# Gate, residual and mean of a layer norm moved into the matmul phases ahead of it

## What is computed

```python
def deepnorm_residual(x, delta, gate, g, b):
    return layer_norm(DEEPNORM_ALPHA * x + gate * delta, g, b)

def layer_norm(x, g, b):
    mu = jnp.mean(xf, axis=-1, keepdims=True)
    var = jnp.mean(jnp.square(xf - mu), axis=-1, keepdims=True)
    return ((xf - mu) * lax.rsqrt(var + LN_EPS)).astype(x.dtype) * g + b

def squared_relu_mlp(h, w_fc1, w_fc2):
    return jnp.square(jax.nn.relu(h @ w_fc1)) @ w_fc2
```

## Time and profile before

| | us |
|---|---|
| median of 3 runs | 5848.92 |
| lowest, highest | 5848.59, 5851.17 |
| the profiled execution | 5849.96 |
| span of its profile | 5848.2 |
| busy: PE, PE's weight loads | 5231.4, 4740.4 |
| busy: DVE, ACT, POOL | 2408.4, 1883.7, 592.0 |

### The profile page before, as it was taken

The page is one execution under the profiler, slowest core; times in us unless marked ns, Lnnn a source line. Parts: engine busy times, 40 slices in busy tenths (PEclk is TensorE's granted clock), DMA queues, the critical chain, the costliest instruction groups (busy, mean ns, idle before and its releaser), DMA issues. The chain is left out here.

```text
span 5848.2 us, 148613 instructions
## 1 busy us (share of the span) xinstructions
PE 5231.4 (89%) x66464; PEld 4740.4 (81%) x66464; DVE 2408.4 (41%) x4332; ACT 1883.7 (32%) x3891; POOL 592.0 (10%) x1104
## 2 busy tenths in 40 slices
PE   6797999988998897999896897899897999988998
PEld 2386888877997876999795776799786888877997
DVE  0242554534334264433324543433452545544334
ACT  1032343433223254222423432322322443433223
POOL 0002232300000000000002221000001232310000
PEclk8798999988998898999897998899898999988999
DMA  9731000011221301221222111122121000011221
GB/s 405 325 116 47 23 15 25 15 57 53 78 72 50 73 2 51 80 72 57 94 99 69 42 36 70 58 73 73 40 104 58 24 15 25 15 43 63 75 72 54
DMA packets 99124, 411.81 MB, mean 70 GB/s; under 512 B 17947, under 2 KB 33691, under 8 KB 68830
## 3 DMA queue, kind: packets, MB, share of 16 engines
q1 hardware_dynamic: 87014, 376.71, 18.5%
q10 hardware_dynamic: 11520, 26.22, 1.1%
HBM read 358.20 MB, written 39.44 MB: 68 GB/s over the span
## 5 line engine op out<-in xcount | busy, mean ns | idle before, releaser
L375 PE MATMUL bank<-src_hi,ring_hi 128*128 128x320 f32 x4032 | 933.1, 313 | 156.8 <-DVE ring_lo L356 58.5
L375 PE MATMUL bank<-src_hi,ring_lo 128*128 128x320 f32 x4032 | 927.1, 311 | 4.0 <-issue 4.0
L375 PE MATMUL bank<-src_lo,ring_hi 128*128 128x320 f32 x4032 | 928.6, 312 | 0.0
L375 PEld LDWEIGHTS bank<-src_hi,ring_hi 128*128 128x128 f32 x4032 | 682.5, 190 | 164.8 <-issue 152.5
L375 PEld LDWEIGHTS bank<-src_hi,ring_lo 128*128 128x128 f32 x4032 | 683.1, 190 | 4.2 <-issue 4.2
L375 PEld LDWEIGHTS bank<-src_lo,ring_hi 128*128 128x128 f32 x4032 | 683.8, 190 | 0.0
L589 ACT ACTIVATE stage<-bank 128x320 f32<-128x320 f32 x512 | 196.1, 435 | 1388.8 <-PE bank L375 1388.8
L367 DVE TENSOR_TENSOR ring_lo<-ring,ring_hi 128x2048 fp32r<-128x2048 f32 x178 | 407.5, 2290 | 519.2 <-ACT ring_hi L363 518.3
L375 PE MATMUL bank<-hidden_hi,ring_hi 128*128 128x320 f32 x2048 | 466.6, 309 | 0.0
L375 PE MATMUL bank<-hidden_hi,ring_lo 128*128 128x320 f32 x2048 | 466.6, 309 | 0.0
L375 PE MATMUL bank<-hidden_lo,ring_hi 128*128 128x320 f32 x2048 | 466.6, 309 | 0.0
(11 more groups left out here) (401 smaller groups left out, 8613.9 us busy)
## 6 DMA issues: line engine op xcount, KB each, us to landing
ring<-w_mlp SPq DMA_DIRECT2D x128, 1024.0 KB, 4.9
mod_ring<-w_mod SPq DMA_DIRECT2D x48, 2048.0 KB, 11.9
ring<-rw_wrkv SPq DMA_DIRECT2D x22, 1024.0 KB, 5.2
rkv<-stage ACTq DMA_DIRECT2D x48, 320.0 KB, 2.2
ring<-dn_win SPq DMA_DIRECT2D x15, 1024.0 KB, 5.2
r_k<-rkv SPq DMA_DIRECT2D x32, 320.0 KB, 3.5
dn_proj<-stage ACTq DMA_DIRECT2D x32, 320.0 KB, 2.2
src<-mixed SPq DMA_DIRECT2D x24, 320.0 KB, 7.3
```

The costliest lines, as they stand in the source:

```text
L375: last = self.nc.tensor.matmul(acc[h][:, 0:HALF], wt[:, n % 2, k, m * P:(m + 1) * P], x[:, k, h * HALF:(h + 1) * HALF], start=first and q ...
```

## The change

1. **Out projection.** A function of its own, `out_projection`, takes the place of `projection` there. It is written out without a loop. ACT gates each unit straight from its banks into `delta`, in three pieces (320, 192 and 128 tokens); DVE forms the residual of the unit at once (`joined`); PE has the mean product of unit u - 2 behind product u. Two pairs of banks hold the units instead of four; two more banks hold the mean and stay until the norm has read them.
2. **Mlp.** The last quarter leaves the loop. In its second half ACT gates block u - 9 behind the evacuation of unit u, DVE joins block u - 10 behind the add of unit u, and PE has the mean product of block u - 10 behind product u. Here too two pairs of banks instead of four.
3. **Norm.** It begins with the subtraction of the mean. A root of one column (`warm`) stands first on ACT, so that the table is loaded there. The memsets, the rounding of the first slab and the two halves of its rest move behind the root, the reciprocal and the scaling.

The parts that carry the work (in the norm, the gates at L684, the residual at L738 and the mean products at L712 are deleted):

```diff
+class Residual:
...
+    def joined(self, past, b):
+        x = self.g.x[:, b, :]
+        return self.nc.vector.scalar_tensor_tensor(x, x, ALPHA if self.first else past[:, b:b + 1], self.delta[:, b, :], ALU.mult, ALU.add)
+
+    def mean_product(self, b):
+        for (cols, n), mean in zip(((S_LAT, LAT), (S_CTX, CTX)), self.mean):
+            self.nc.tensor.matmul(mean[:, 0:n], self.g.mean_w, self.g.x[:, b, cols], start=(b == 0), stop=(b == NB - 1))
+
+def out_projection(nc, g, w, delta, layer, mean, load):
...
+            @block.tensor
+            def _(pe):
+                def means(b):
+                    pe.wait_ge(s["joined"], b + 1)
+                    residual.mean_product(b)
...
+                            last = ring.product(acc[u % DEEP], n, m, k, x_hi, x_lo, k == 0, k == NB - 1)
+                        last.then_inc(s["mm_done"], 1)
+                        if u >= 2:
+                            means(u - 2)
+                for b in range(NB - 2, NB):
+                    means(b)
...
+                        act.wait_ge(s["mm_done"], u + 5)
+                        front, back = acc[u % DEEP]
+                        residual.gated(delta[:, u, 0:HALF], front[:, 0:HALF], past, u, 0)
+                        residual.gated(delta[:, u, HALF:LAT], back[:, 0:in_half], past, u, 0)
+                        residual.gated(delta[:, u, LAT:T], back[:, in_half:HALF], past, u, 1).then_inc(s["evacuated"], 1)
...
+                    for u in (2 * n, 2 * n + 1):
+                        dve.wait_ge(s["evacuated"], u + 1 + DEEP)
+                        residual.joined(past, u).then_inc(s["joined"], 1)
+def mlp(nc, g, w, delta, held, layer, mean):
...
                             last.then_inc(s["mm_done"], 1)
+                            if final and u >= NB + 2:
+                                means(u - NB - 2)
...
+                block_(LAST, False, True)
+                for b in range(NB - 2, NB):
+                    means(b)
...
                             last.then_inc(s["evacuated"], 1)
-
-                with act.Fori(0, QUARTERS - 1) as i:
+                            if not more and u > NB:
+                                gate(u - NB - 1)
...
                                 nc.vector.tensor_tensor(delta[:, u - NB, :], delta[:, u - NB, :], row,
                                                         ALU.add).then_inc(s["added"], 1)
+                                if not more and u >= NB + 2:
+                                    join(u - NB - 2)
...
@@ norm @@
+                nc.scalar.activation(warm[:, :], g.eps_ln, ACT.Sqrt).then_inc(s["warm"], 1)
                 for b in range(NB):
                     act.wait_ge(s["centred"], b + 1)
                     nc.scalar.activation(dl[:, b, :], g.x[:, b, :], ACT.Square).then_inc(s["squares"], 1)
                 act.wait_ge(s["variances"], 1)
                 nc.scalar.activation(dev[:, :], var[:, 0:W], ACT.Sqrt, bias=g.eps_ln).then_inc(s["deviation"], 1)
+                if held:
+                    act.wait_ge(s["w_first"], 16)
+                    nc.scalar.copy(hi, raw).then_inc(s["w_upper"], 1)
```

More of the change, by code:

```diff
@@ L451, in _ @@
                 for b in range(NB):
[L452 to L456, removed]
+                    for ap, cols in token_parts(g.h, b):
                         last = nc.scalar.copy(x_hi[:, b, cols], ap)
                     last.then_inc(s["hi_ready"], 1)
[L459 to L465, removed]
+                    if b in (2, 3):
+                        ring.upper_first(act, (FRONT, BACK)[b - 2])
                 def block_(i, more):
@@ L523, in mlp @@
+def mlp(nc, g, w, delta, held, layer, mean):
     QUARTERS, PER = NFB // NB, 8
-    names = SPLIT_SEMS + ["cleared", "added", "link", "hidden"]
-    PASS_UNITS = 2 * PER
+    names = SPLIT_SEMS + ["cleared", "added", "link", "hidden", "past_cols", "gated", "joined"]
+    PASS_UNITS, DEEP, LAST = 2 * PER, 2, QUARTERS - 1
+    residual = Residual(nc, g, delta, layer, 1, mod_at(layer, 5), mean)
     with buffers(nc) as (sb, banks), phase(nc, *names) as s:
@@ L530, in mlp, with _ @@
         stage = sb("stage", 2, T)
-        bank = banks(8)
-        acc = [(bank[2 * u], bank[2 * u + 1]) for u in range(UNITS)]
+        past = sb("past", 2 * NB)
+        bank = banks(2 * DEEP)
+        acc = [(bank[2 * u], bank[2 * u + 1]) for u in range(DEEP)]
         with nc.Block() as block:
+            @block.gpsimd
+            def _(pool):
+                residual.past_columns(past).then_inc(s["past_cols"], 1)
             @block.sync
@@ L575, in _, with gate @@
                     last.then_inc(s["hi_ready"], 1)
+                def gate(b):
+                    act.wait_ge(s["added"], NB * QUARTERS + b + 1)
+                    for c, cols in enumerate((S_LAT, S_CTX)):
+                        last = residual.gated(delta[:, b, cols], delta[:, b, cols], past, b, c)
+                    last.then_inc(s["gated"], 1)
                 def block_(i, more):
@@ L607, in _, with join @@
                 dve.wait_ge(s["cleared"], 1)
+                def join(b):
+                    dve.wait_ge(s["gated"], b + 1)
+                    residual.joined(past, b).then_inc(s["joined"], 1)
                 def block_(i, more):
@@ L709, in _ @@
                 for b in range(NB):
-                    pe.wait_ge(s["added"], b + 1)
-                    for cols, mean, n in parts:
-                        last = nc.tensor.matmul(mean[:, 0:n], g.mean_w, g.x[:, b, cols], start=(b == 0), stop=(b == NB - 1))
-                last.then_inc(s["sums"], 1)
-                for b in range(NB):
                     pe.wait_ge(s["squares"], b + 1)
@@ L733, in _ @@
                 last.then_inc(s["chosen"], 1)
-                if not first:
-                    dve.wait_ge(s["past_cols"], 1)
-                for b in range(NB):
-                    dve.wait_ge(s["gated"], b + 1)
-                    nc.vector.scalar_tensor_tensor(g.x[:, b, :], g.x[:, b, :], ALPHA if first else past[:, b:b + 1], dl[:, b, :],
-                                                   ALU.mult, ALU.add).then_inc(s["added"], 1)
-                dve.wait_ge(s["sums"], 1)
-                for b in range(NB):
-                    for cols, mean, n in parts:
-                        last = nc.vector.tensor_tensor(g.x[:, b, cols], g.x[:, b, cols], mean[:, 0:n], ALU.subtract)
-                    last.then_inc(s["centred"], 1)
+                dve.wait_ge(s["deviation"], 1)
+                nc.vector.reciprocal(dev[:, :], dev[:, :]).then_inc(s["root"], 1)
                 if held:
```

199 lines of the change are left out of this document (133 added, 66 removed).

## The result

The changed kernel took 5883.7 us (median of 5 runs, 5873.2 to 5886.7) beside 5848.6 of the kernel before on the same chip: a ratio of **1.0055, 95% interval 1.0043 to 1.0068**, 32 us slower. The profiled execution took 5886.7 us, its span is 5884.5, 36.3 us more than in the profile of before.

The account below looks back on a forecast made before the run. TensorE, busy 89% of the span, was taken as the bound. The eight norms' 125.1 us became 42.0 (out projections) plus 128.8 (mlps), +45.7, less 4.8 for jumps: +41 us, so 5890 us, range 5862 to 5915.

Parts of the forecast that it names:

- the clock: Mlp last quarters: TensorE's clock halves after two stalls in three, 1.1 us a stall, 6.6 us a norm (0 to 10.2).
- the switches: TensorE changing between products and mean weights: 12 a norm, between 0 and 2.3 us, taken as 0.4 us a norm.
- the stall with the product behind it: Mlp: 2.61 us of idle TensorE at each of six units, plus a 1.08 us mean product; five before the last product.
- the jumps: Mlp loops: four jumps back instead of eight leave one gap of two, -4.8 us (bounds -9.6 to +9.6).
- Output projection: Four out projections with their norms: no wait between units, 5.4 + 4.5 = 9.9 us a norm; 20 us won.
- The tail: From a phase's last product to the end of its mean: 4.5 us in the out projection, 6.8 us in the mlp.
- the gate in three pieces: ScalarE's gate of the out projection's last unit from its banks: 1.5 us, bounds 0.77 to 1.65.
- Neither bound: Mlp clock loss: 0 to 1.7 us a stall, from no fall (5864, chance 0.13) to every stall halving it (5905).
- The table load: Norms behind the out projections: early load wins 0.43 us, but squares start 0.6 us later; net +0.2 us each.
- do not catch up: Same four norms: squares starting 0.6 us late stay late, at 0.79 us each with VectorE feeding at 0.81.
- The moved work: Norm and mlp: moved cast of first weights, five memsets and two accumulators instead of four cost nothing.
- The rival that the mlp is covered too: Mlp: join of unit u - 2 done before product u ends, 11.7 us a norm, 5808 us; chance 0.05.

Follow-up runs that it names:

- one moved line: Changed kernel with the mlp's mean product one unit later, 5802.8 us; or with VectorE's join ahead of its wait for the new unit, 5803.0 us.

## Why the prediction was right, point by point

The forecast was 5890 us within 5862 to 5915; the measured time is 5883.7, the measured difference 32 us (25 to 40) where 41 were forecast, just above its interval. The mechanism is the one forecast: the same stalls, in the same number, at the same place. The sizes are in part off, and in part they cancel. Set against the 36.8 us of the stages, the clock and the switches were put 9 us too high, the stall with the product behind it 3.5 and the jumps 2 us too low.

- **Output projection**: forecast 20 us won (21 by its stage, less the table), measured 19.9. The tail was forecast at 4.5 us and is 4.5 to 4.8; the gate in three pieces takes 1.37 us, in the bounds and near the 1.5 taken. It didn't wait between its units.
- **The stall in the mlp**: forecast 2.61 us at six units of four norms, some 62 us in all; measured 2.51 and 60.2. VectorE's add and join overlap, 0.74 us from start to start and not 0.85. But the distance of the evacuations is 10.90 us, not the 10.7 forecast: a stalled mean product adds 3.86 us to its unit, where 2.61 + 1.08 = 3.69 were forecast. A pause of 2.51 us so costs 0.27 more than its length. In the records 0.10 of that is in the mean product itself (1.35 us long at 1833.07, 1.24 at 1342.52 in the output projection, where nothing pauses); the rest is that matmuls which follow each other overlap (those of a unit are 0.31 us long and 0.15 apart), and the last one ahead of a pause has none to overlap with. The tail was forecast at 6.8 us and is 6.84 in two norms; in the two others a half clock in it makes it 8.5.
- **The clock**: two falls in three were taken, one in two is measured: 12 of 24, 4.7 us a norm and not 6.6. Filling the stall removed all of them, which shows that the idle time is their cause. Neither bound came, no fall or a fall each time. With the mlps alone changed it was 9 of 24, so the share is itself not a fixed one, and 6.6 was a middle between bounds and not a mechanism. The rule of the Trainium skill, TensorE: Matmul & The Clock Gate, section on psum-queue depth-cycling, is that micro-idles between groups of matmuls make the clock fall and rise. By the trace it holds in kind, but not for every stall, and not at all for pauses of 1.3 us.
- **Switches**: forecast 0.4 us a norm; the output projection's units are 8.12 us apart, which leaves nothing for them.
- **The table load**: forecast 0.2 us lost in each of four norms, measured 0.43 won. The step that failed is "do not catch up": 0.79 us a square was VectorE's pace, not ScalarE's. Back to back they start 0.62, 0.63 and 0.68 us apart, and with the fourth they have caught up. The page ScalarE: Activation LUTs of the Trainium skill, section What ACT_TABLE_LOAD costs, has back-to-back instructions overlap by about 0.09 us, and the trace agrees (0.72 long, 0.62 to 0.63 apart in the first ones). Its 2.66 us for a switch is seen in no run here; where the load stands ahead of the root, squares, load and root follow each other within 0.03 us.
- **The jumps**: one gap at the jumps was forecast for 4.8 us less; there was one, but it cost 6.8 us in place of the 9.6 of the two before, so 2.8 us less. That it was one was luck: taking a rate from two gaps of one program was the weak step, for four other programs had none, and the one with the output projections alone had two, each of two pauses of 1.1 to 1.4 us.
- **The moved work** (first slab, memsets, two pairs of banks) cost nothing, as forecast: from the root to the scaling the norms take 4.24 us as before, and from there to the mlp's first product 12.6.

The rival that the mlp is covered too gave 5808 us. It isn't what the changed kernel does, but it is what one moved line makes of it: 5802.8 and 5803.0.

## What to carry to other kernels

When work is woven into another engine's queue, it isn't its own inputs that count but what stands ahead of them in the queue of the engine that makes them: here a residual whose gated input was ready one unit before (its gate ended at 1832.44, the next evacuation began at 1841.50) came 2.5 us late because it was made behind the newest unit. Take from the producer's queue only what it finished before the consumer's current unit began, one unit of lag more, or put the old work ahead of the wait for the new. And count a pause of TensorE above its length: each of 2.5 us here cost 0.27 us more and, in nearly half of the cases, 1.5 to 1.7 us of clock.

## What the runs showed of the hardware

- A pause of 2.51 us in dense products brought TensorE's clock down 12 times of 24 in the changed kernel and 9 times of 24 with the mlps alone changed; one of 1.34 us at the same places 0 times of 24, and one filled with needless products 0 times of 24. A fall is 3.4 us at 1.2 GHz and cost 1.5 to 1.7 us.
- An f32 mean product of 640 columns adds 1.08 us to a dense row of products (units 8.12 us apart, not 7.04). Behind a pause of 2.51 us, pause and product add 3.86 us (10.90 apart), 0.27 more than the two lengths.
- TensorE can pause at the jump back of a long loop (768 matmuls a pass), twice within a few us and 1.0 to 3.0 us each, in one of four loops with the same body and in seven of eleven programs: costs of 4.4, 5.2 and 6.8 us with the clock's fall. The one program with the loop written out had none. Why that one loop, and whether the loop is the cause, is not settled.
- In layers that were not touched the time differs by several us between programs: the DeltaNet layer ahead of its output projection took 810 to 820 us. A change's parts measured apart therefore need their stages' times beside the whole.
